# Softmax pairs of a hybrid encoder: the next pair's scores move behind the odd gate

## The reference

```
branch = jnp.einsum('btnw,nwd->btnd', o, w_branch)
gate = jax.nn.sigmoid((xn @ w_gate).reshape(B, T, N_BRANCH, D_MODEL))
return jnp.einsum('btnd,btnd->btd', gate, branch) @ w_out, new_rows
```

## Time and profile before

| | |
|---|---|
| median of three runs | 2085.11 us |
| profiled execution | 2086.56 us, span 2084.8 us |
| TensorE, VectorE, ScalarE, GpSimd busy | 99%, 67%, 48%, 11% |
| granted clock of TensorE | 0.999 |
| TensorE's share of the chain that ended last | 96% |

### The profile page before, as it was taken

How to read it: one execution, slowest core, us unless ns; L and a number is a source line. 1 busy time by engine, 2 the same in 40 slices (tenths; PEclk the granted TensorE clock), 3 DMA queues, 4 the chain that set the end, 5 groups by cost and what they waited for, 6 DMA issues and landing times.

```text
span 2084.8 us, 39646 instructions
## 1 busy us (share of the span) xinstructions
PE 2071.7 (99%) x15860; PEld 1969.0 (94%) x15860; DVE 1390.1 (67%) x2606; ACT 1005.8 (48%) x1635; POOL 234.9 (11%) x174
## 2 busy tenths in 40 slices
PE   9999999999999999999999999999999999999998
PEld 8888989998999999999998989899989999999998
DVE  7658786788737763676465786777787477536653
ACT  6267315647527652444352672265565366424433
POOL 0023000000040110011300220000001311001112
PEclk9999999999999999999999999999999999999999
DMA  6231323121222222222232212221212222232222
GB/s 205 79 107 41 92 83 106 52 72 52 61 89 82 82 89 94 81 82 90 91 111 81 96 42 92 81 98 61 72 52 72 71 91 81 90 92 84 87 88 92
DMA packets 54344, 175.21 MB, mean 84 GB/s; under 512 B 7076, under 2 KB 11860, under 8 KB 54212
## 3 DMA queue, kind: packets, MB, share of 16 engines
q1 hardware_dynamic: 47364, 158.88, 24.6%
q0 software_dynamic: 3072, 10.11, 1.2%
q10 hardware_dynamic: 3776, 4.34, 0.6%
HBM read 160.25 MB, written 12.90 MB: 83 GB/s over the span
## 4 chain that ended last, share of the span: by engine, by line
PE 96%; DVE 2%; ACT 1%; issue 0%; DMA 0%; SPq 0%; DVEq 0%
PE d L1522 63%; PE d L1576 14%; PE ab L1622 4%; PE d L1914 2%; PE d L1587 2%; PE d L1923 2%; PE ab L1863 1%; PE ab L1851 1%; PE d L1626 1%; PE ab L1900 1%; PE ab L1522 1%; PE ab L1677 0%; PE d L1768 0%; PE ab L1708 0%; PE ab L1718 0%; DVE w L900 0%
## 5 line engine op out<-in xcount | busy, mean ns | idle before, releaser
L489 ACT ACTIVATE wh<-raw 128x512 fp32r<-128x512 f32 x548 | 345.0, 631 | 715.8 <-PE d L1522 556.9
L861 DVE TENSOR_TENSOR wl<-raw,wh 128x512 fp32r<-128x512 f32 x548 | 389.8, 713 | 282.3 <-ACT wh L489 273.7
L1522 PE MATMUL d<-xh,wh 128*128 128x288 f32 x2400 | 511.7, 294 | 2.1 <-DVE xl L874 1.1
L1522 PE MATMUL d<-xl,wh 128*128 128x288 f32 x2400 | 509.1, 293 | 0.0
L1522 PE MATMUL d<-xh,wl 128*128 128x288 f32 x2400 | 509.0, 293 | 0.0
L1522 PEld LDWEIGHTS d<-xh,wh 128*128 128x128 f32 x2400 | 381.3, 188 | 7.7 <-issue 5.7
L1522 PEld LDWEIGHTS d<-xl,wh 128*128 128x128 f32 x2400 | 381.4, 188 | 0.0
L1522 PEld LDWEIGHTS d<-xh,wl 128*128 128x128 f32 x2400 | 381.4, 188 | 0.0
L1576 PE MATMUL d<-xh,wh 128*128 128x288 f32 x768 | 173.8, 308 | 0.0
L1576 PE MATMUL d<-xh,wl 128*128 128x288 f32 x768 | 164.8, 296 | 0.0
L1576 PE MATMUL d<-xl,wh 128*128 128x288 f32 x768 | 164.5, 295 | 0.0
(11 more groups left out here) (325 smaller groups left out, 3264.5 us busy)
## 6 DMA issues: line engine op xcount, KB each, us to landing
raw<-in_w SPq DMA_DIRECT2D x286, 512.0 KB, 3.5
out_o_k<-k POOLq DMA_DIRECT2D x4, 1152.0 KB, 7.2
out_o_v<-v POOLq DMA_DIRECT2D x4, 1024.0 KB, 8.9
x<-in_xT SPq DMA_DIRECT2D x8, 288.0 KB, 5.7
k<-in_bc_k_past ACTq DMA_DIRECT2D x4, 512.0 KB, 4.4
v<-in_bc_v_past ACTq DMA_DIRECT2D x4, 512.0 KB, 5.4
out_y<-z SPq DMA_DIRECT2D x4, 432.0 KB, 2.7
raw<-in_w SPq DMA_DIRECT2D x4, 256.0 KB, 6.0
```

What stands on the lines that cost most here:

```text
L489: act.activation(wh[:, c % SPLIT_SLOTS, :], stored, ACT.Copy).then_inc(high_done, 1)
L861: dve.tensor_tensor(lows, stored, highs, ALU.subtract).then_inc(low_done, 1)
L1522: ins = pe.matmul(outs[half], w_, r_[:, kk, HALF * half:HALF * half + HALF], start=first and n == 0 and begin, stop=last and n == len(kks) ...
```

## The change

On TensorE the scores of the next pair for stages 0 and 1 move from ahead of the odd gate's blocks 4 to 7 to behind them, directly ahead of `values(p)`. On VectorE, from the second pair on, the weight chunk cg + 2 and the odd gate's `gate_take` now come first, and then the maxima of stages 0 and 1. ScalarE, GpSimd and SyncE are unchanged.

```
                         if p:
+                            low_parts(l, cg + 2)
+                            gate_take(l, m, 2 * p - 1)
                             max_step(l, m, p, 0)
-                            low_parts(l, cg + 2)
                             if m == A:
                                 mask_step(l, p, 1)
-                                gate_take(l, m, 2 * p - 1)
                                 masked_max(l, p, 1)
                                 o = take_output(l, m, p - 1)
                             else:
                                 max_step(l, m, p, 1)
-                                gate_take(l, m, 2 * p - 1)
                             scale_step(l, m, p, 0)
...
                             turn(3)
+                            gate_blocks(l, m, 2 * p + 1, range(4, 8))
                             if p < PAIRS - 1:
                                 scores_wide(p + 1)
                                 scores_next(p + 1)
-                            gate_blocks(l, m, 2 * p + 1, range(4, 8))
```

## The result

The changed kernel takes 2091.70 us (median of 8 runs), the kernel before 2086.22 us (8 runs beside it): a ratio of 1.0028, 95% interval 1.0019 to 1.0037. That is 5.5 us slower, where 6.2 us had been forecast.

A forecast was written before the change was run, and what follows sets the result against it. TensorE, busy 2071.7 of 2084.8 us, was taken as the bound. Waits of 3.4 us in mixer C and 2.8 us in A add 6.2 us to the 2085.11 us median: forecast 2091.3 us, range 2084.0 to 2096.0.

The forecast's parts named there:

- Start of the scores: On TensorE in C, the next pair's scores start 3.19 us later, behind the odd gate's last four blocks.
- First mask in C: On VectorE in C, the first mask starts at 344.01 instead of 342.09, 1.92 us late.
- Second exponential and what hangs on it: In C, the second maximum, ScalarE's second exponential, chunk cg+3 and take_output all come 1.32 us late.
- The cover: In C, the next pair's first transposes have 0.76 us of usable room before TensorE waits for take_output.
- A: In mixer A, the odd gate's weights load 0.46 us later in each of six hand-overs, 2.8 us in all.
- The unknown row: On TensorE, scores directly ahead of values may cost a 0.17 us gap or nothing; neither counts while the transposes wait.
- Sum: Over both mixers' hand-overs, 3.4 us in C and 2.8 us in A make 6.2 us slower.
- The rule of the Trainium skill: On TensorE, changing tiling mode drains it; three changes instead of four would alone save twelve times 0.17, 2.0 us.
- Rival (a): Scores-to-transposes chain some 0.5 us shorter, so TensorE never waits: 2083.1 us, or 2081.1 without a scores-values gap; chance 0.13.
- rival (b): Only one mixer waits: C alone gives 2087.5 us, A alone 2086.9 us; chance 0.12.
- rival (c): Each pair waits twice, another 0.5 us or so on each of twelve hand-overs, 2097.3 us; chance 0.08.

The follow-up runs named there:

- act_early: The changed kernel with ScalarE rounding chunk cg+3 between the first and second exponential from the second pair on; 2084.57 us, ratio 0.9991 to the kernel before.
- c_only: The change made in mixer C alone, with A keeping both old orders of the kernel before; 2089.77 us, ratio 1.0020.
- dve_only: The kernel before with only VectorE's new order, TensorE keeping its old one; 2120.62 us, ratio 1.0160.
- pe_only: The kernel before with only TensorE's new order, VectorE keeping its old one; 2102.69 us, ratio 1.0080.
- c_take: The changed kernel with VectorE's take_output moved ahead of chunk cg+3 in mixer C, nothing done for A; 2089.45 us, ratio 1.0016.

## Why the prediction was right

The mechanism, the two places that cost, both releasers and the size came as forecast. By its steps, with times counted from T3, which starts at 339.24 us in this execution, 0.19 us later than before:

- **Start of the scores.** G takes 342.84 - 339.48 = 3.36 us, as forecast. The scores start 342.84 - 0.19 - 339.47 = 3.18 us later than before; forecast 3.19.
- **First mask in C.** 344.23 - 0.19 - 342.09 = 1.95 us late; forecast 1.92.
- **Second exponential and what hangs on it.** 347.95 - 0.19 - 346.40 = 1.36 us late, take_output 1.35 us; forecast 1.32. ScalarE's round of cg + 3 did carry the lateness on: move it forward, and the wait is gone (act_early).
- **The cover.** 0.76 us in C were worked out. T0's weights load at 351.84 - 0.19 = 351.65, 0.58 us later than the 351.07 of the earlier trace rows; forecast 0.56. The list puts these waits at 0.5 us each, where 0.6 to 0.75 had been named; that is the idle time of the matmuls, and the idle time of the weight loading is 0.74. The runs with extra instructions agree with the cover: 0.67 us fit under it, and from 1.34 us T0 came 0.57 late.
- **A.** 0.53 us a hand-over, forecast 0.46: the mechanism is right, the term is 0.07 us short. Of that 0.05 is the mask, which started 1.18 us behind the start of the scores rather than the 1.13 us taken from the modelled ends in C. Whether T0 waits in A had been left open: it does, 0.10 us for the scaling. As the prediction argued, that wait did not add to the one at the gate's bank, for the whole hand-over lost 0.53 us.
- **The unknown row.** Scores directly ahead of values show a gap of 0.21 us, just above the upper of the two bounds. As forecast it counts only where nothing waits.
- **Sum.** C 0.54 and A 0.53 us, six times each: 6.4 us in the pairs, forecast 6.2. The spans differ by 5.3 us only, since the profile of before had lost 1.29 us elsewhere.
- **The rule of the Trainium skill** (TensorEngine Tiling (Array Packing), Tiling Modes), that a change of tiling mode drains TensorE. By it alone the time would have fallen by 2.0 us. act_early, where only the short wait of T0 in A is left, shows that part: 6 x 0.21 + 6 x 0.09 = 1.8 us, under a third of the 6.4 us that the same step cost. So one change of mode fewer goes with the gain that was worked out. That the change of mode is what makes the gap is not shown: within the scores, all on 64 rows, the weight loading has gaps of the same kind, 0.23 us at 343.38 and 0.33 us at 343.81 of the changed kernel, and the time line marks none from the values to the even gate, where the mode changes.

Rival (a), a cover that holds, is refuted by the waits; rival (b) by waits in both mixers, and by c_only, which has about half the loss. Of rival (c) one sign came, the wait of T0 in A, but not its price: a hand-over in A lost 0.53 us, not 1.0.

## What to carry to other kernels

Where an engine is busy throughout and the list of waits is empty at a place, the question to put to the profile is not what can be won there but how late each feeding chain may become before the empty list fills: take the last step of the chain that the engine needs, subtract its end from the time of need, and compare with the delay that the edit puts at the chain's head. A gain on the full engine that is bought with a later start of a chain has to be paid from that cover; here 0.2 us were bought with 1.3 us where 0.8 were free. The repair is to take out of the chain what does not belong to it (a weight chunk standing between two exponentials and the next copy), on whichever engine that is easiest.

## What the runs showed of the hardware that was not expected

**The clock after a longer wait.** In dve_only the waits of 2.26 us for take_output were followed, at four of the six hand-overs in C, by a stretch at lower clock. The windows around the second one of the first layer (same columns as above; the clock is the third figure from the right):

```profile
372.00:376.00 4.00, 4.00 (x52) 3.93 (x49) 3.93 (x8) 2.32 (x8) 0.00 (x0) 1.00 0.01 4
376.00:380.00 4.00, 1.74 (x14) 1.43 (x12) 2.44 (x8) 3.51 (x10) 0.00 (x0) 0.97 0.18 28
380.00:384.00 4.00, 4.00 (x20) 3.04 (x19) 2.63 (x5) 1.81 (x3) 0.00 (x0) 0.60 0.26 103
384.00:388.00 4.00, 4.00 (x37) 3.51 (x36) 1.76 (x6) 2.64 (x7) 0.00 (x0) 1.00 0.00 0
```

A mean of 0.60 is a stretch mostly at the lower of the two levels, 1.2 GHz, and then 2.4 GHz again. It fell at the second and third hand-over of C in the first layer and at the first and second in the second layer; at the other two, after waits of the same length, it stayed at 1.00. The span grew by 33.2 us and the waits by 25.5, which leaves 7.7 us. As an estimate from the windows, each fall cost about 1.7 us of full-speed time (4 us at 0.97 and 4 us at 0.60, or at 0.88 and 0.69), four of them 6.9 us; TensorE's busy time, 2079.3 us for the same instructions, is 7.6 us above that of the earlier trace rows. The waits of up to 1.5 us in pe_only and 0.6 us in the changed kernel left the clock at 0.999.

**Two paces of the same matmuls.** C's first run of projections, 336 matmuls of 128x288 without a wait and at full clock, takes 43.73 us in some executions and 44.84 us in others. In one profile of before it took the one in the first layer and the other in the second (pieces of the chain that ended last: start, us, what):

```profile
227.69 43.73 PE d L1522 x336
...
1259.73 44.84 PE d L1522 x336
```

c_take had 44.84 in both layers, act_early and the changed kernel 43.73 in both. With what stands behind it, it moves the stretch by 1.29 us, as much as a fifth of the change under study. What sets the pace stays open. It is why the account above is made by stretches and not by whole spans.
